# A hybrid decoder layer whose large products read their moving operand back to front

## The reference

```python
h = rms_norm(x, ln_mix_pre)
y = hybrid_mixer(h, ...)             # h @ w_in, four mixers, gates, w_branch, w_out
x = x + rms_norm(y, ln_mix_post)
h = rms_norm(x, ln_mem_q)
y = memory_cross_attention(h, rms_norm(mem, ln_mem_kv), mem_wq, mem_wkv, mem_wo)
x = x + rms_norm(y, ln_mem_post)
h = rms_norm(x, ln_ffn_pre)
y = conv_ffn(h, ffn_w_up, ffn_conv_w, ffn_conv_b, ffn_w_down)     # 2048 -> 2 x 5632 -> 2048
x = x + rms_norm(y, ln_ffn_post)
```

## Time and profile before

| | |
|---|---|
| median of three runs | 2194.74 us (2193.69 to 2195.88) |
| the profiled execution, its own time | 2193.37 us |
| its span, first to last instruction | 2191.6 us |
| busy: TensorE matmuls / weight loads | 2166.9 us (99%) / 1847.8 us (84%) |
| busy: VectorE / ScalarE / GpSimd | 1439.2 us (66%) / 1065.0 us (49%) / 244.6 us (11%) |
| mean granted TensorE clock | 0.998 of full speed |
| HBM traffic over the span | 179 GB/s |

### The profile page before, as it was taken

How to read it: one execution, slowest core, us unless ns; L and a number is a source line. 1 busy time by engine, 2 the same in 40 slices (tenths; PEclk the granted TensorE clock), 3 DMA queues, 4 the chain that set the end, 5 groups by cost and what they waited for, 6 DMA issues and landing times.

```text
span 2191.6 us, 33212 instructions
## 1 busy us (share of the span) xinstructions
PE 2166.9 (99%) x12606; PEld 1847.8 (84%) x12606; DVE 1439.2 (66%) x1651; ACT 1065.0 (49%) x1438; POOL 244.6 (11%) x220
## 2 busy tenths in 40 slices
PE   8999999999999999999999999989999999999998
PEld 6888888788888888888888888878888888888887
DVE  7985658667554545467765544578777777876444
ACT  6452344545444444445444444566555555644443
POOL 1132000000000101025110001411111111100000
PEclk9999999999999999999999999999999999999999
DMA  7543344345666666675556543536555655566664
GB/s 265 177 150 115 119 146 157 129 157 185 193 192 192 192 192 191 193 265 182 187 180 198 190 151 122 189 118 206 187 182 194 188 190 181 193 191 212 193 192 152
DMA packets 107071, 393.83 MB, mean 180 GB/s; under 512 B 11888, under 2 KB 12144, under 8 KB 106576
## 3 DMA queue, kind: packets, MB, share of 16 engines
q1 hardware_dynamic: 106672, 391.10, 55.5%
q10 hardware_dynamic: 288, 1.18, 0.2%
HBM read 390.14 MB, written 2.10 MB: 179 GB/s over the span
## 4 chain that ended last, share of the span: by engine, by line
PE 94%; DVE 3%; ACT 1%; DMA 1%; issue 0%; SPq 0%; DVEq 0%; ACTq 0%
PE bank L1008 24%; PE bank L1017 13%; PE bank L543 7%; PE sm L430 5%; PE sm L429 5%; PE sm L427 5%; PE bank L546 4%; PE bank L1221 3%; PE bank L1223 3%; PE bank L1222 3%; PE bank L427 2%; PE bank L430 2%; PE bank L429 2%; PE sm L595 2%; PE bank L1105 1%; PE bank L1104 1%
## 5 line engine op out<-in xcount | busy, mean ns | idle before, releaser
L1977 DVE TENSOR_TENSOR part<-part,part 128x1024 fp32r<-128x1024 f32 x724 | 933.5, 1292 | 528.8 <-ACT part L1274 517.2
L1274 ACT ACTIVATE part<-part 128x1024 fp32r<-128x1024 f32 x724 | 763.7, 1057 | 579.2 <-PE sm L430 177.6
L1008 PE MATMUL bank<-part,part 128*128 128x512 f32 x2336 | 562.3, 392 | 0.0
L1008 PEld LDWEIGHTS bank<-part,part 128*128 128x128 f32 x2336 | 428.8, 188 | 83.1 <-issue 0.4
L1017 PEld LDWEIGHTS bank<-part,part 128*128 128x128 f32 x2336 | 300.0, 191 | 11.8
L1017 PE MATMUL bank<-part,part 128*128 128x256 f32 x2336 | 303.6, 283 | 0.0
L543 PE MATMUL bank<-part,part 128*128 128x512 f32 x832 | 207.3, 396 | 0.6 <-DVE part L2032 0.5
L427 PE MATMUL sm<-part,part 128*128 128x512 f32 x512 | 199.2, 389 | 0.0
L429 PE MATMUL sm<-part,part 128*128 128x512 f32 x512 | 199.2, 389 | 0.0
L430 PE MATMUL sm<-part,part 128*128 128x512 f32 x512 | 199.2, 389 | 0.0
L543 PEld LDWEIGHTS bank<-part,part 128*128 128x128 f32 x832 | 151.5, 188 | 32.9 <-issue 2.1
(11 more groups left out here) (382 smaller groups left out, 2203.5 us busy)
## 6 DMA issues: line engine op xcount, KB each, us to landing
part<-in_w_up SPq DMA_DIRECT2D x176, 512.0 KB, 4.5
part<-in_w_gate SPq DMA_DIRECT2D x128, 512.0 KB, 4.6
part<-in_w_dn SPq DMA_DIRECT2D x88, 512.0 KB, 4.4
part<-in_w_br SPq DMA_DIRECT2D x40, 512.0 KB, 4.6
part<-in_w_out SPq DMA_DIRECT2D x32, 512.0 KB, 4.6
part<-in_w_mk SPq DMA_DIRECT2D x32, 512.0 KB, 4.5
part<-in_w_mv SPq DMA_DIRECT2D x32, 512.0 KB, 4.5
part<-in_w_q SPq DMA_DIRECT2D x32, 512.0 KB, 4.4
```

The lines of the kernel that those rows point to most:

```text
L1008: mm = pe.matmul(dst, w[:, 0, k, :], x[:, k0 + k, :], start=start and k == 0, stop=stop and k == n - 1, skip_group_check=True)
L1274: act.activation(wsplit[(2 * m + h) % 4][:, 0, 0:n, :], raw[:, m % 2, h, 0:n, :], cp) .then_inc(sem("hi_done"), 1)
L1977: tt(w[:, 1, 0:n, :], raw[:, m % 2, h, 0:n, :], w[:, 0, 0:n, :].bitcast(f32), SUB).then_inc(sem("lo_done"), 1)
```

## The change

In ten lines, all in matmuls, the moving operand is read with a step of -1 instead of +1 along its columns. So that each result still lands in its own column, the PSUM output of the first four functions is written with a step of -1 as well. In the down projection the output keeps its order, and instead the columns of each block of 512 of `w_down` are stored in reverse in HBM by the host's layout, so that reading them backwards gives them in their own order. No instruction, semaphore, buffer or transfer is added, removed or moved.

```diff
# token_half
-                    pe.matmul(dst, xh, w[:, 0, j, :], start=first and h == 0 and j == 0, stop=False,
+                    pe.matmul(dst[:, ::-1], xh, w[:, 0, j, ::-1], start=first and h == 0 and j == 0, stop=False,
                               skip_group_check=True)
-                    pe.matmul(dst, xh, w[:, 1, j, :], start=False, stop=False, skip_group_check=True)
-                    mm = pe.matmul(dst, xl, w[:, 0, j, :], start=False, stop=last and h == 1 and j == 1,
+                    pe.matmul(dst[:, ::-1], xh, w[:, 1, j, ::-1], start=False, stop=False, skip_group_check=True)
+                    mm = pe.matmul(dst[:, ::-1], xl, w[:, 0, j, ::-1], start=False, stop=last and h == 1 and j == 1,
                                    skip_group_check=True)
...
# mix_half
-                            mm = pe.matmul(b, w[:, 0, k, :], H[:, 8 * h + k, :], start=h == 0 and k == 0,
+                            mm = pe.matmul(b[:, ::-1], w[:, 0, k, :], H[:, 8 * h + k, ::-1], start=h == 0 and k == 0,
...
-                            mm = pe.matmul(b[:, T:2 * T], w[:, 1, k, :], H[:, 8 * h + k, 0:T], start=False, stop=False,
+                            mm = pe.matmul(b[:, T:2 * T][:, ::-1], w[:, 1, k, :], H[:, 8 * h + k, 0:T][:, ::-1], start=False, stop=False,
...
# high_products
-                    mm = pe.matmul(dst, w[:, 0, k, :], x[:, k0 + k, :], start=start and k == 0,
+                    mm = pe.matmul(dst[:, ::-1], w[:, 0, k, :], x[:, k0 + k, ::-1], start=start and k == 0,
...
# low_products
-                    mm = pe.matmul(dst[:, T:2 * T], w[:, 1, k, :], x[:, k0 + k, 0:T], start=False,
+                    mm = pe.matmul(dst[:, T:2 * T][:, ::-1], w[:, 1, k, :], x[:, k0 + k, 0:T][:, ::-1], start=False,
...
# values_half (the other two lines alike)
-                    pe.matmul(bank[:, s, :], x, w[:, 0, j, :], start=k == 0, stop=False, skip_group_check=True)
+                    pe.matmul(bank[:, s, ::-1], x, w[:, 0, j, ::-1], start=k == 0, stop=False, skip_group_check=True)
...
# down_half (the other two lines alike)
-                    pe.matmul(bank[:, s, :], x, w[:, 0, j, :], start=k0 + j == 0, stop=False, skip_group_check=True)
+                    pe.matmul(bank[:, s, :], x, w[:, 0, j, ::-1], start=k0 + j == 0, stop=False, skip_group_check=True)
...
# the host's layout
-    a["w_dn"] = wide(x["ffn_w_down"][0])
+    a["w_dn"] = wide(x["ffn_w_down"][0].reshape(FFN, -1, 4 * P)[:, :, ::-1].reshape(FFN, D))
```

More of the change, by code:

```diff
@@ L1103, in values_half @@
                     x = X2[:, k, s * P:(s + 1) * P]
-                    pe.matmul(bank[:, s, :], x, w[:, 0, j, :], start=k == 0, stop=False, skip_group_check=True)
-                    pe.matmul(bank[:, s, :], x, w[:, 1, j, :], start=False, stop=False, skip_group_check=True)
-                    mm = pe.matmul(bank[:, s, :], X2[:, k, T + s * P:T + (s + 1) * P], w[:, 0, j, :], start=False,
+                    pe.matmul(bank[:, s, ::-1], x, w[:, 0, j, ::-1], start=k == 0, stop=False, skip_group_check=True)
+                    pe.matmul(bank[:, s, ::-1], x, w[:, 1, j, ::-1], start=False, stop=False, skip_group_check=True)
+                    mm = pe.matmul(bank[:, s, ::-1], X2[:, k, T + s * P:T + (s + 1) * P], w[:, 0, j, ::-1], start=False,
                                    stop=k == KT - 1, skip_group_check=True)
@@ L1220, in down_half @@
                     x = g[:, k + j, s * P:(s + 1) * P]
-                    pe.matmul(bank[:, s, :], x, w[:, 0, j, :], start=k0 + j == 0, stop=False, skip_group_check=True)
-                    pe.matmul(bank[:, s, :], x, w[:, 1, j, :], start=False, stop=False, skip_group_check=True)
-                    mm = pe.matmul(bank[:, s, :], g[:, k + j, T + s * P:T + (s + 1) * P], w[:, 0, j, :], start=False,
+                    pe.matmul(bank[:, s, :], x, w[:, 0, j, ::-1], start=k0 + j == 0, stop=False, skip_group_check=True)
+                    pe.matmul(bank[:, s, :], x, w[:, 1, j, ::-1], start=False, stop=False, skip_group_check=True)
+                    mm = pe.matmul(bank[:, s, :], g[:, k + j, T + s * P:T + (s + 1) * P], w[:, 0, j, ::-1], start=False,
                                    stop=k0 + j == FT - 1, skip_group_check=True)
```

## The result

The changed kernel takes 2228.15 us (median of four runs, 2226.71 to 2228.41) against 2194.22 us for the kernel before (four runs): the ratio is 1.0152, with an interval of 1.0135 to 1.0170. It is slower by 34 us, 1.5%.

A forecast was written before the change was run, and what follows sets the result against it. The prediction took TensorE's distances between matmul starts to bound the kernel. Profiled 2193.37 us + 0 for the read + 0 for the write, set 1.4 us higher by the runs' median, gave 2194.7 us; 8-in-10 range 2130 to 2320 us.

The forecast's parts named there:

- What bounds the kernel: Whole kernel: TensorE's matmuls cover 2166.9 of 2191.6 us, so time is the sum of distances between matmul starts.
- any change of the distance goes through to the end nearly whole: Up projection: VectorE and ScalarE keep slack, so a changed matmul distance reaches total time; 10.0 us per nanosecond on each.
- The write with step -1: PSUM outputs of all changed matmuls but the down projection's: taken as 0, bounded above by +1557 us.
- the doubt about PSUM: Falling PSUM writes might count as non-contiguous and run at half rate, giving 3752 us.
- The read with step -1: Moving operand of all changed matmuls: taken as 0, bounded by -113 us and +1781 us.
- The split into a fixed and a column term: Every changed matmul: distance is a fixed 14.7 ns plus 0.414 ns a column.
- the prediction's own sign: If only 512-column matmuls, or only those with moving weights, moved, the split into fixed and column term had failed.
- the prediction's 14.7 ns: Each matmul: the fixed part of the distance, 226.7 ns less 512 columns at 0.414 ns.
- Rival 3: Each reversed matmul starts later, same rate per column: up to +147 us, 2342 us; named value 2268 us; chance 0.12.
- Rivals 1 and 2: Half rate for falling PSUM writes (3752 us, chance 0.07) or for falling moving reads, down projection included (3976 us, chance 0.08).
- Rival 4: The fixed term of each reversed matmul shrinks: down to 2082 us, half of it 2138 us; chance 0.10.

The follow-up runs named there:

- e4: Kernel before with all operands read forward and the outputs of the four functions written backward: 2193.78 us, ratio 0.9999.
- e1_forms: Kernel before plus 14 groups of 32 unused matmuls varying read, write and width; 512 columns: forward 226.6 ns, read backward 233.4, written backward 227.2.
- e12: Kernel before plus unused 512-column matmuls, moving operand alone shifted 0 to 32 elements: forward 226.8 to 235.7 ns, backward 233.2 to 239.6.
- e13: Kernel before plus unused 512-column matmuls, stationary operand alone shifted: forward 232.9 ns at 8 elements, backward 233.2 to 233.6 at every place.
- e16: Kernel before plus unused forward 512-column matmuls, both operands shifted alike (226.8 to 228.2 ns at 8 to 64 elements) or one alone by 64 or more (226.4 to 226.8).
- e2: Kernel before with only the 256-column matmuls at L546 and L1017 reversed, read and write: 2185.72 us against 2193.81, ratio 0.9963.
- e5: Kernel before plus 18 groups of 32 unused matmuls varying the stationary operand; 512 columns, 128 stationary: forward 226.6 ns, backward 233.4, alternating directions 230.3.
- e11: Kernel before plus groups of 32 unused matmuls with bfloat16 operands: 512 columns 215.9 ns both ways, 256 columns 109.1 forward and 109.4 backward.
- e6_widths: Kernel before plus 21 groups of 24 unused matmuls, 64 to 508 columns, both directions: backward minus forward -0.4 ns at 224 columns, +4.2 at 448.

## Why the prediction was wrong

*What bounds the kernel* was right, and so was "any change of the distance goes through to the end nearly whole": 33.7 us by distances, 33.2 us of span.

*The write with step -1: 0.* Right (e4, e1_forms), and the doubt about PSUM was unfounded. The Trainium skill ("Advanced Engine Details and Errata", PSUM Cachelines), which was cited for the doubt, says that any non-contiguous pattern slows matmuls down; a falling write does not count as one here: 227.2 ns against 226.6.

*The read with step -1: "I take 0".* This is the step that failed. It is 6.8 ns on a matmul of 512 columns by itself, 6.5 ns in the token orientation, 4.3 ns in the channel orientation, and -1.2 to -1.6 ns on one of 256. The reason given was that the duration of the earlier trace rows was the same "from three different buffers". But in this kernel all these buffers, tiles and slices stand at multiples of 128 elements to each other, and in the groups of e12, e13 and e16 that is the relative place where the forward read of 512 columns is fast. The three rows looked like three cases and were one. What is left of a forward distance after 512 columns at 2.4 GHz (213.3 ns) is 13.5 ns at place 0 and up to 24.9 ns at others (226.8 to 238.2 ns); for the backward read it was never below 19.8 ns (233.1 to 239.6).

*The split into a fixed and a column term* failed with it, by the prediction's own sign: only the matmuls of 512 columns got longer. It was used to price rivals 3 and 4. Its slope is right for the forward read only at that place, and only roughly: from 256 to 320 columns 27.2 ns, 0.425 a column. With bfloat16 the remainder at 512 columns is 215.9 - 213.3 = 2.6 ns against 13.3 for float32r, so the prediction's 14.7 ns do not belong to each matmul; the plain float32 row pointed there and I used it only as a bound.

*Rival 3*, a later start of each reversed matmul, comes nearest in size: 10.0 us a nanosecond x 3.4 ns mean gives the 34 us. But its own mark, 512 and 256 columns longer by the same nanoseconds, is not there, and blocks of 256 and 128 columns read backward, which start much nearer to the front, cost the same (e1). Rivals 1 and 2 overstate the cost some fifty times: a falling step halves no rate. Rival 4 named the gain that e2 found at 256 columns, for a reason that the alternating group of e5 does not bear out; the larger part of that gain is on the untouched wide matmuls.

The Trainium skill ("SBUF — State Buffer", Specifications) was cited for a backward read keeping its hits per line; e11 agrees with it for bfloat16 (215.9 both ways), the float32r groups of e1 do not (226.6 against 233.4). The Trainium skill ("TensorE: Matmul & The Clock Gate", Step-by-step) says that the port of the weight load is independent of the moving operand's and that loading the next weights takes no read bandwidth from the running matmul. e13 speaks against it for float32r: moving only the stationary operand by 8 elements takes the forward distance from 226.8 to 232.9 ns.

*What stays open.* That the two reads interact is shown; which part of the memory they meet in is not, nor why a falling moving read has no fast place among those tried, nor why 320 columns show no difference. Another direction of the stationary read was not tried. The gain of e2 is measured (8.1 us), its cause is only narrowed: forward, 128 stationary columns cost 6 ns over 64 there, backward 0.3.

## What to carry to other kernels

Before a row is used as evidence that something does not matter, ask whether that something varies among the rows; here no trace of the kernel could show an effect of place. With float32r operands and 512 columns, keep moving and stationary slices at multiples of 64 elements to each other and read forward; other widths are worth a measurement of their own. A reversed output, a reversed order of blocks, and with bfloat16 a reversed read, cost nothing at the places tried. Matmuls of 256 columns between forward ones of 512 may be worth reading backward: 0.4% here, for two lines.

## What the runs showed of the hardware that was not expected

In a row of short matmuls without a gap the clock fell. In e6_widths, two groups of 64 columns, two of 128 and two of 192 follow the 512-column matmuls with PE busy throughout. The rows are from the groups of 64, of 128 and, last, from 192 and 224:

```profile
2188.00:2191.00 3.00, 3.00 (x29) 3.00 (x29) 2.96 (x5) 0.00 (x0) 0.00 (x0) 1.00 0.15 64
2193.00:2201.00 8.00, 8.00 (x39) 8.00 (x39) 0.00 (x0) 0.00 (x0) 0.00 (x0) 0.50 0.02 6
2209.00:2213.00 4.00, 4.00 (x38) 4.00 (x38) 0.00 (x0) 0.00 (x0) 0.00 (x0) 1.00 0.00 0
```

At 0.50, 1.2 GHz, a matmul of 128 columns stood 215.4 ns from the next, as one of 192 did (215.4), with the weight loads busy for 8.00 of 8.00 us. So there the weight load very likely sets the distance. The clock came back during the second group of 192 columns, whose matmuls do not differ from those of the group before. This was seen in one run, and what the fall hangs on was not tested. A forward read of 512 columns being slower with fewer stationary columns (226.6, 230.0, 231.6 ns for 128, 64, 32) was the other surprise.
